# A block kernel's long convolution: transforms split into even and odd tokens, half of the frequencies multiplied, the tables in one ring chunk

## The reference

```python
def hyena_branch(cols, p):
    w = p['hy_conv_w']
    u = w[0] * shift_prev(cols) + w[1] * cols + w[2] * shift_next(cols) + p['hy_conv_b']
    x0, x1, v = jnp.split(u, 3, axis=-1)
    z = v * x1
    z = long_conv(z, hyena_filter_spectrum(cols.shape[1], p)) + p['hy_bias'] * z
    return z * x0

def long_conv(z, spec):
    L = z.shape[1]
    zf = jnp.fft.rfft(z.astype(jnp.float32), n=2 * L, axis=1)
    return jnp.fft.irfft(zf * spec, n=2 * L, axis=1)[:, :L].astype(z.dtype)
```

## Time and profile before

| what | us |
|---|---|
| median of three runs | 3726.84 (3725.3 to 3729.33) |
| span of the profiled execution | 3725.3 |
| time of the fastest run | 3725.3 |
| TensorE busy | 3401.7 (91%) |
| VectorE busy | 1142.7 (31%) |
| ScalarE busy | 599.9 (16%) |
| start of the filter-spectrum matmuls | 798.80 |
| start of the first matmul of `mix_branches` | 887.93 |
| DMA rate in the expert stage | 417 GB/s mean |

### The profile page before, as it was taken

One profiled execution on the slowest core, in us unless ns is written; L12 is line 12 of the kernel. 1 busy time (PEld: TensorE's weight loads), 2 busy tenths in 40 slices (PEclk: granted clock), 3 DMA queues, 4 the chain that ended last, 5 costly groups with the idle time before them and its releaser, 6 DMA issues. The chain is left out here.

```text
span 3725.3 us, 48323 instructions
## 1 busy us (share of the span) xinstructions
PE 3401.7 (91%) x21329; PEld 1687.3 (45%) x21329; DVE 1142.7 (31%) x1977; ACT 599.9 (16%) x1192; POOL 8.0 (0%) x40
## 2 busy tenths in 40 slices
PE   6978999999996988889899899999999977999998
PEld 3557878444444333323333344454444444444443
DVE  2255565432113000000000226644665032222211
ACT  2134322110011000000000212242121012211100
POOL 0000000000000000000000000000000000000000
PEclk9989999999997999999999999999999988999999
DMA  6134444211226999999999521103433234212220
GB/s 239 45 125 169 149 162 162 87 45 45 90 76 269 430 429 431 430 430 428 427 427 430 205 72 63 51 7 80 144 121 138 80 110 162 86 68 68 69 95 34
DMA packets 197654, 668.77 MB, mean 180 GB/s; under 512 B 31048, under 2 KB 95036, under 8 KB 171205
## 3 DMA queue, kind: packets, MB, share of 16 engines
q1 hardware_dynamic: 196456, 665.31, 45.8%
q10 hardware_dynamic: 989, 0.36, 0.0%
HBM read 640.97 MB, written 22.31 MB: 178 GB/s over the span
## 5 line engine op out<-in xcount | busy, mean ns | idle before, releaser
L2718 PE MATMUL banks<-h_T,weight_ring 128*128 128x512 f32 x1408 | 612.7, 596 | 5.9 <-PEq L90 5.9
L2718 PEld LDWEIGHTS banks<-h_T,weight_ring 128*128 128x128 f32 x1408 | 267.5, 191 | 337.7 <-issue 337.7
L2020 PE MATMUL banks<-weight_ring,xe_T 128*64 128x512 f32 x1312 | 296.9, 599 | 41.3 <-DMA weight_ring<-in_exp_w 39.4
L2730 PE MATMUL banks<-weight_ring,ffn_act 128*128 128x512 f32 x704 | 302.5, 592 | 0.0
L2816 DVE SCALAR_TENSOR_TENSOR conv<-banks,cols,conv 128x510 f32<-128x510 f32 (+1 forms) x176 | 131.8, 749 | 341.2 <-ACT conv L2786 336.6
L2730 PEld LDWEIGHTS banks<-weight_ring,ffn_act 128*128 128x128 f32 x704 | 133.8, 190 | 168.4 <-issue 168.4
L2020 PEld LDWEIGHTS banks<-weight_ring,xe_T 128*64 128x64 f32 x1312 | 90.2, 137 | 235.2 <-issue 160.0
L2036 PE MATMUL banks<-weight_ring,hid_T 128*64 128x512 f32 x656 | 146.7, 596 | 9.5 <-DMA weight_ring<-in_exp_w 9.5
L2786 ACT ACTIVATE conv<-banks,cols 128x512 f32<-128x512 f32 x88 | 63.6, 772 | 503.3 <-PE banks L2718 503.3
L2341 PE MATMUL banks<-h_T,weight_ring 128*128 128x512 f32 x320 | 142.0, 597 | 0.0
L2020 PE MATMUL banks<-h_T,xe_T 128*64 128x512 f32 x464 | 105.4, 596 | 17.7 <-DMA h_T<-in_exp_w 17.7
(11 more groups left out here) (579 smaller groups left out, 4135.3 us busy)
## 6 DMA issues: line engine op xcount, KB each, us to landing
weight_ring<-in_exp_w SPq DMA_DIRECT2D x123, 2048.0 KB, 15.7
h_T<-in_exp_w SPq DMA_DIRECT2D x41, 2048.0 KB, 15.7
weight_ring<-in_ada_w SPq DMA_DIRECT2D x24, 2048.0 KB, 8.7
weight_ring<-in_ffn_w_up SPq DMA_DIRECT2D x44, 1024.0 KB, 6.3
expert_out<-in_exp_w SPq DMA_DIRECT2D x19, 2048.0 KB, 19.0
weight_ring<-in_mod_w SPq DMA_DIRECT2D x12, 2048.0 KB, 8.5
weight_ring<-in_ffn_w_down SPq DMA_DIRECT2D x10, 2048.0 KB, 7.8
spare<-in_exp_w SPq DMA_DIRECT2D x9, 2048.0 KB, 20.5
```

Source lines behind the costliest of these rows:

```text
L2020: mm = pe.matmul(k.ps[64 * half:64 * half + 64, 2 * c + b % 2, :], R.rows[:, e // 2 % 2, kt, (e % 2) * CAP:(e % 2 + 1) * CAP], w[:, r, 512 ...
L2718: mm = pe.matmul(k.ps[:, b + c, :], w[:, c, kt, m * P:m * P + P], hT[:, kt, :], start=kt == 0, stop=kt == 7)
L2730: return pe.matmul(k.ps[:, 2 * t + n, :], out[:, kt, t * P:t * P + P], src[:, n * 512:n * 512 + 512], start=kt == 0, stop=kt == FF_T - 1)
```

## The change

The tokens are sorted into even and odd ones. A transform's values at a frequency and at its mirror image differ only in the sign with which the odd tokens enter, so the matmuls are done for the lower 256 frequencies alone, for even and odd tokens apart, and sums and differences of the two parts give both halves.

- **Tables**: `k_dft` has 256 frequencies instead of 512, its rows (and those of the window and the features) in the order even tokens, odd tokens; `k_inverse` has 256 rows. Together they fill one chunk of 2 MB, so the stage takes 4 chunks instead of 5 and every later chunk moves up by one.
- **TensorE**: `half_sums` does 4 parts (cosine even, sine odd, cosine odd, sine even) x 2 tiles of tokens = 8 matmuls for each of 2 tiles of frequencies, for the filter and for z. The transposes read every second token. `back` does the inverse with 256 columns per matmul, even and odd output tokens apart, part of it while VectorE is still at the second tile of frequencies.
- **ScalarE** copies two banks at a time (`crossed`), for the filter and now also for z.
- **VectorE** makes sums and differences (spectrum, `z_parts`), scales, and does the products in `multiply`, on halves of the channels: first the two products' parts, then the sums and differences that the even and the odd half of the inverse need. The output is written in two interleaved halves per channel tile.
- **Banks**: the projection uses banks 0 to 3 (before 0, 2, 4, 6), the filter's network 4 to 7. The chunk of tables is given back when the last inverse matmul is done (before: `k_dft` after the products, `k_inverse` at the end).

The core of the diff (left out: the numbering of the events, and the new bank numbers of the projection, the network and the norm):

```diff
-    w = TWO_PI * (np.arange(L)[None, :] + 0.5) / (2 * L)
-    cos, sin = np.cos(w * n), np.sin(w * n)
+    w = TWO_PI * (np.arange(L // 2)[None, :] + 0.5) / (2 * L)
+    split = np.concatenate([np.arange(0, L, 2), np.arange(1, L, 2)])
+    cos, sin = np.cos(w * n)[split], np.sin(w * n)[split]
...
-        "k_inverse": f(np.stack([cos.T / L, -sin.T / L])), "k_window": f(window),
-        "k_feat": f(feat.T), "k_misc": f(misc), "k_pick": f(pick),
+        "k_inverse": f(np.stack([cos.T / L, -sin.T / L])), "k_window": f(window[split]),
+        "k_feat": f(feat.T[:, split]), "k_misc": f(misc), "k_pick": f(pick),
...
-    out += [[(I["k_dft"][c].rearrange("(k p) n -> p k n", p=P), [P, 4, 512]) for c in range(2)]]
-    out += [[(I["k_inverse"][c].rearrange("(k p) n -> p k n", p=P), [P, 4, 512]) for c in range(2)]]
+    out += [[(I["k_dft"][c].rearrange("(k p) n -> p k n", p=P), [P, 4, 256]) for c in range(2)] +
+            [(I["k_inverse"][c].rearrange("(k p) n -> p k n", p=P), [P, 2, 512]) for c in range(2)]]
...
-    bank = lambda i: 2 * (i % 4)
+    bank = lambda i: i % 4
...
-        spec = sb("filter_spectrum", [P, 2, LT, HY_W])
+        spec = sb("filter_spectrum", [P, 2, 4, HY_W])
+        Z, Q = sb("z_spectrum", [P, 4, HY_W]), sb("spectrum_products", [P, 4, HY_W])
-        ztok, sumdif, prod, scr, window = u[:, 4:8, :], filt, filt, absum, spec[:, 0, :, :]
+        ztok, sumdif, scr, window = u[:, 4:8, :], filt, absum, spec[:, 0, :, :]
+        prod, crossed = filt, absum
+        first_banks, late_banks = (4, 5, 6, 7), (0, 1, 2, 3)
...
-            k.ring.load_ahead(sync, 5)
+            k.ring.load_ahead(sync, 4)
...
-            dft = k.ring.chunk(3).rearrange("p (c t n) -> p c t n", c=2, t=LT)
+            dft = k.ring.chunk(3)[:, 0:2048].rearrange("p (c t n) -> p c t n", c=2, t=LT)
+            inv = k.ring.chunk(3)[:, 2048:4096].rearrange("p (c k n) -> p c k n", c=2, k=2)
+            def half_sums(kt, banks, source):
+                for b, (c, odd) in zip(banks, ((0, 0), (1, 1), (0, 1), (1, 0))):
+                    for t in range(2):
+                        mm = pe.matmul(k.ps[:, b, :], dft[:, c, 2 * odd + t, kt * P:kt * P + P], source(c, 2 * odd + t), start=t == 0, stop=t == 1)
+                return mm
             pe.wait_ge(dve_done, dve_n[("sumdif", LT - 1)])
-            order = (1, 3, 5, 7, 0, 2, 4, 6)
-            for c in range(2):
-                for kt in range(LT):
-                    if c:
-                        pe.wait_ge(dve_done, dve_n[("sums", 8 + kt)])
-                    for t in range(LT):
-                        mm = pe.matmul(k.ps[:, order[4 * c + kt], :], dft[:, c, t, kt * P:kt * P + P], sumdif[:, c, t, :],
-                                       start=t == 0, stop=t == LT - 1)
-                    ev(("spectrum", c, kt), mm)
+            ev(("spectrum", 0), half_sums(0, first_banks, lambda c, t: sumdif[:, c, t, :]))
             pe.wait_ge(dve_done, dve_n[("z", HY_T - 1)])
+            ev(("spectrum", 1), half_sums(1, late_banks, lambda c, t: sumdif[:, c, t, :]))
+            pe.wait_ge(dve_done, dve_n[("spectrum", 0)])
             for t in range(LT):
-                pe.wait_ge(act_done, act_n[("spectrum", 0, t)])
                 for j in range(HY_T):
-                    mm = pe.transpose(k.ps[:, order[t], j * P:j * P + P], u[:, 8 + j, t * P:t * P + P], k.sq("eye"))
+                    mm = pe.transpose(k.ps[:, first_banks[t], j * P:j * P + P], u[:, 8 + j, bass.DynSlice(t // 2 + 256 * (t % 2), P, step=2)], k.sq("eye"))
                 ev(("turned", t), mm)
+            pe.wait_ge(dve_done, dve_n[("spectrum", 1)])
             pe.wait_ge(act_done, act_n[("turned", LT - 1)])
-            for kt in range(LT):
-                for c in range(2):
-                    for t in range(LT):
-                        mm = pe.matmul(k.ps[:, (order[4:] + order[:4])[2 * kt + c], :], dft[:, c, t, kt * P:kt * P + P], ztok[:, t, :],
-                                       start=t == 0, stop=t == LT - 1)
-                ev(("z", kt), mm)
-            k.ring.wait(pe, 4)
-            inv = k.ring.chunk(4).rearrange("p (c t n) -> p c t n", c=2, t=LT)
+            ev(("z", 0), half_sums(0, late_banks, lambda c, t: ztok[:, t, :]))
+            ev(("z", 1), half_sums(1, first_banks, lambda c, t: ztok[:, t, :]))
+            def back(j, kt, odd):
+                for c, part in ((0, 2 * odd), (1, 1 if odd else 3)):
+                    mm = pe.matmul(k.ps[:, j + 4 * odd, 0:256], prod[:, kt, part, j * P:j * P + P], inv[:, c, kt, 256 * odd:256 * odd + 256],
+                                   start=(c, kt) == (0, 0), stop=(c, kt) == (1, 1))
+                return mm
+            for odd in range(2):
+                if odd:
+                    pe.wait_ge(dve_done, dve_n["z_parts_late"])
+                for j in range(HY_T):
+                    pe.wait_ge(dve_done, dve_n[("prod", 0, j // 2)])
+                    back(j, 0, odd)
             for j in range(HY_T):
-                for kt in range(LT):
-                    if j == 0:
-                        pe.wait_ge(dve_done, dve_n[("prod", max(kt, j))])
-                    for c in range(2):
-                        mm = pe.matmul(k.ps[:, order[4 + j], :], prod[:, c, kt, j * P:j * P + P], inv[:, c, kt, :],
-                                       start=(c, kt) == (0, 0), stop=(c, kt) == (1, LT - 1))
-                ev(("y", j), mm)
+                pe.wait_ge(dve_done, dve_n[("prod", 1, j // 2)])
+                back(j, 1, 0)
+                ev(("y", j), back(j, 1, 1))
...
-            for c in range(2):
-                for kt in range(LT):
-                    act.wait_ge(pe_done, pe_n[("spectrum", c, kt)])
-                    ev(("spectrum", c, kt), act.activation(spec[:, c, kt, :], k.ps[:, (1, 3, 5, 7, 0, 2, 4, 6)[4 * c + kt], :], ACT.Copy))
+            crossing = lambda banks: k.ps[:, banks[2]:banks[2] + 2, :]
+            act.wait_ge(dve_done, dve_n[("sumdif", LT - 1)])
+            act.wait_ge(pe_done, pe_n[("spectrum", 0)])
+            ev(("spectrum", 0), act.activation(crossed[:], crossing(first_banks), ACT.Copy))
+            act.wait_ge(pe_done, pe_n[("spectrum", 1)])
+            act.wait_ge(dve_done, dve_n[("spectrum", 0)])
+            ev(("spectrum", 1), act.activation(crossed[:], crossing(late_banks), ACT.Copy))
             for t in range(LT):
                 act.wait_ge(pe_done, pe_n[("turned", t)])
-                ev(("turned", t), act.activation(ztok[:, t, :], k.ps[:, (1, 3, 5, 7)[t], :], ACT.Copy))
+                ev(("turned", t), act.activation(ztok[:, t, :], k.ps[:, first_banks[t], :], ACT.Copy))
+            act.wait_ge(dve_done, dve_n[("spectrum", 1)])
+            act.wait_ge(pe_done, pe_n[("z", 0)])
+            ev(("z", 0), act.activation(crossed[:], crossing(late_banks), ACT.Copy))
+            act.wait_ge(pe_done, pe_n[("z", 1)])
+            act.wait_ge(dve_done, dve_n["z_parts"])
+            ev(("z", 1), act.activation(crossed[:], crossing(first_banks), ACT.Copy))
...
-            for c in range(2):
-                for kt in range(LT):
-                    dve.wait_ge(act_done, act_n[("spectrum", c, kt)])
-                    ev(("scaled", c, kt), dve.tensor_tensor(spec[:, c, kt, :], spec[:, c, kt, :], inv_norm[:], ALU.mult))
-            for kt in range(LT):
-                dve.wait_ge(pe_done, pe_n[("z", kt)])
-                zr, zs = (k.ps[:, (0, 2, 4, 6, 1, 3, 5, 7)[2 * kt + c], :] for c in range(2))
-                hr, hi = spec[:, 0, kt, :], spec[:, 1, kt, :]
-                link(dve.tensor_tensor(scr[:, 0, :], zs, hi, ALU.mult))
-                link(dve.tensor_tensor(scr[:, 1, :], zs, hr, ALU.mult))
-                link(dve.tensor_tensor(prod[:, 0, kt, :], zr, hr, ALU.mult))
-                link(dve.tensor_tensor(prod[:, 1, kt, :], zr, hi, ALU.mult))
-                link(dve.tensor_tensor(prod[:, 0, kt, :], prod[:, 0, kt, :], scr[:, 0, :], ALU.add))
-                ev(("prod", kt), dve.tensor_tensor(prod[:, 1, kt, :], prod[:, 1, kt, :], scr[:, 1, :], ALU.subtract))
-            dve.sem_inc(k.ring.used, 1)
+            direct = lambda banks: k.ps[:, banks[0]:banks[0] + 2, :]
+            for kt, banks in enumerate((first_banks, late_banks)):
+                dve.wait_ge(act_done, act_n[("spectrum", kt)])
+                H = spec[:, kt]
+                dve.tensor_tensor(H[:, 0:2, :], direct(banks), crossed[:], ALU.add)
+                ev(("spectrum", kt), dve.tensor_tensor(H[:, 2:4, :], direct(banks), crossed[:], ALU.subtract))
+                ev(("scaled", kt), dve.tensor_tensor(H, H, bcast(inv_norm[:], 4), ALU.mult))
+            pairs = lambda ap: (ap[:, bass.DynSlice(0, 2, step=2), :], ap[:, bass.DynSlice(1, 2, step=2), :])
+            def z_parts(kt, banks, name):
+                dve.wait_ge(act_done, act_n[("z", kt)])
+                dve.tensor_tensor(Z[:, 0:2, :], direct(banks), crossed[:], ALU.add)
```

(43 more changed lines are left out.)

15 lines of the change are left out of this document (7 added, 8 removed).

## The result

The changed kernel takes 3698.96 us (median of four runs, 3696.78 to 3700.0), the kernel before beside it 3726.07 (four runs, 3721.69 to 3729.33): ratio 0.9921, 95% interval 0.9908 to 0.9934, so 27.1 us less.

A forecast was written before the change was run, and what follows sets the result against it. TensorE was taken to bound the stretch: 41.2 us of matmuls removed, 13.7 given back to VectorE, 2.8 to the clock, leaving 24.7, taken as 24.5. That gave 3700.8, 3702.3 as a median; range 3694 to 3713, own range 3699 to 3706.

The forecast's parts named there:

- TensorE's work: Filter spectrum, transform of z and inverse each lose 13.7 us of matmul time, 41.2 in sum.
- The new wait before z: After the transposes, the transform of z waits about 2.1 us for VectorE, in place of 0.90.
- VectorE sets the end: From z's first results, VectorE's products (5.47 per `multiply`) and outputs set the end; 13.7 given back, gain 27.5 us.
- The barrier: Between hyena's outputs and the mix: VectorE ends at 858.3, the mix starts at 860.4; the earlier trace had 2.08.
- The clock: TensorE's clock falls in the inverse's last two tiles, costing 1.9 us, plus 0.9 at the mix: 2.8 together.
- The edits costing nothing: New bank numbers, one chunk of tables and SyncE's reordered queue cost nothing; the expert stage starts earlier and takes as long.
- The first: Rival: the clock never falls more than before; gain 27.5 us (3697.8), up to 29.3. Chance 14%.
- The second: Rival: the clock falls ahead of the transform of z too; gain 19 to 23 us, 3702 to 3706. Chance 14%.
- The rule of the page: Transposes don't count as TensorE busy, so z's transform would begin at 1.2 GHz; sum 22.7 instead of 24.5 us.
- The third: Rival: matmuls of 256 columns cost as much as 512, slowing inverse and outputs; 3705 to 3709 us. Chance 2%.
- the fourth: Rival: the gain is lost in the expert stage, its loads beginning no earlier; 3725 us. Chance 3%.
- the fifth: Rival: slower, through patterned VectorE instructions in `multiply`; at three times their price 3741.6 us. Chance 2%.

The follow-up runs named there:

- z_twice: Changed kernel with the transform of z computed twice (its 32 records become 64): 3700.74 us, stretch from filter transform to mix 66.65 against 58.72.
- inverse_twice: Changed kernel with 16 more matmuls of 256 columns (6.9 us) in the first half of the inverse: 3696.67 us, stretch 58.78 against 58.72.
- parts_reordered: Changed kernel, doing first those parts of z's transform that need neither the last transposed tile nor VectorE's second difference: 3690.04 us, stretch 57.25 against 58.72.
- linked_products: Changed kernel with each VectorE instruction of `z_parts` and `multiply` waiting for the one before, 18 more links: 3695.5 us, stretch 60.99, 2.27 more.
- returned_late: Changed kernel with the tables' slot given back after the last output instead of ahead of it: 3695.85 us, stretch 59.66, 0.94 more.
- two_chunks: Changed kernel with the tables in two ring chunks of 1 MB again, 5 chunks for the stage: 3691.25 us, stretch 58.85, 0.13 more.
- more_transposes: Changed kernel with the 16 transposes of z done five times (80 records): 3704.56 us, stretch 65.53, 6.81 more.
- filled_lull: Changed kernel with four matmuls that nobody reads between the first output and the barrier: 3699.93 us, stretch 58.74, first mix block 13.81 instead of 15.50.
- changed_again: The changed kernel itself, compared again in five rounds: 3695.32 us against 3725.52 for the kernel before, ratio 0.992, stretch 58.73.
- sums_on_tensor: Changed kernel with two sums of `multiply`, for the first tile of frequencies, left to TensorE (16 more matmuls): 3692.84 us, stretch 56.36, 2.36 less.
- no_final_sums: Changed kernel without the last sum and difference of each `multiply`, so the inverse reads unfinished products: 3686.41 us, stretch 53.40, 5.3 less.

## Why the prediction was right, and where it was short

**The mechanism held.** The time lies 3.3 below the forecast of 3702.3, inside the range, 0.04 under the forecast's own range of 3699 to 3706; the second comparison (3695.32) lies further below. The gain was under-forecast: 24.7 worked out, 30.3 between the two spans. The span was to be 3700.8 and is 3695.0, 5.8 less; the median comes out closer because it lies 4.0 above the span, where 1.5 was added. That part is luck. The likeliest way was the right one, with its clock term too large.

**TensorE's work: right.** 32 records took 13.7 instead of 64 taking 27.5, and the 256-column records are 0.215 apart at full clock. 41.2 went, and z_twice and inverse_twice show which of TensorE's work still counts: that ahead of the first products, and not the inverse.

**The new wait before z: right.** The release is VectorE's second difference, which ends 817.07 - 799.65 = 17.4 after the stage's start where 17.5 was worked out. The wait is 1.67 instead of 2.1, since 16 transposes take 2.07 instead of 1.7. parts_reordered, which removes it, gets 1.47 back.

**VectorE sets the end: right; its pace was mis-sized.** The first sums of z start 25.83 after the stage's start, as worked out (25.8). From there "1.22 + 6 x 0.69, with three linked waits of 0.035" gave 5.47 for one `multiply`, and it measured 5.12; the sums 2.39 instead of 2.48; an output tile 1.64 instead of 1.73. The step added lengths, and unlinked instructions overlap by 0.08. That is 4 x 0.35 + 2 x 0.09 = 1.6 to the end of the products, and 0.3 in the outputs. linked_products shows the effect by itself: 2.27 for 18 links.

**The barrier: wrong by 1.07.** The sum kept the 2.08 of the earlier trace rows between VectorE's last end and the mix. Now it is 858.37 - 857.36 = 1.01. Before, SyncE issued the gate chunk at 885.94, just behind VectorE's end at 885.85, and reached the barrier 1.0 later. The prediction saw that "its 1.0 of issuing ends near 856", and failed to take it out of the 2.08. returned_late puts it back: 0.94.

**The clock: the event right, its price wrong.** The granted clock did fall inside the inverse, and again behind the barrier. Stretches of the changed kernel:

```profile
838.00:842.00 4.00, 3.88 (x10) 3.15 (x11) 3.93 (x5) 0.00 (x0) 0.00 (x0) 0.57 0.01 4
859.00:862.00 3.00, 3.00 (x5) 1.35 (x4) 0.00 (x0) 0.61 (x1) 0.00 (x0) 0.50 1.09 387
862.00:870.00 8.00, 8.00 (x19) 3.42 (x18) 0.00 (x0) 0.00 (x0) 0.00 (x0) 1.00 0.13 46
```

But it fell at 838, not in the last two tiles. The 24 records there take 7.13 instead of 24 x 0.215 = 5.2, TensorE is still early for the next products by 0.37, and VectorE doesn't notice: of the 1.9, nothing is on the path. At the mix the loss is the old one: 15.67 in both kernels. So the 2.8 came to 0.

Together, for the stretch: 1.9 (clock) + 1.6 + 0.3 (VectorE) + 1.07 (barrier) = 4.8 to 4.9. It was to be 89.13 - 27.5 + 1.9 = 63.5, and 58.72 is 4.8 less. The 0.9 for the mix is the rest.

**The edits costing nothing: right.** two_chunks shows it for the layout, the timelines for SyncE's queue and the expert stage; the distance from the mix's start to the end moved by 0.8, within the bound of 3.

**Rivals.** The first (no loss by the clock) named a gain of 27.5. It was right that the clock costs nothing more than before, but for the wrong reason: the clock fell, and it was hidden. That 27.5 lies near the 27.1 between the medians is luck, as the stretch gained 30.4. The second has fallen: the transform of z took 14.00 for 32 records, as the filter's did (13.90). The rule of the page has fallen with more_transposes. The third is excluded by 0.215; the fourth by 2836.6; the fifth by `multiply` at 5.12, with no pattern of 2 x 256 or 4 x 256 slower than a plain one.

**Where the scatter is seen.** In the changed kernel and its variants with one chunk of tables, all code ahead of the filter transform is the same, and yet that transform's first records lie between 795.6 and 803.2. 680 to 690 us, first before, then after:

```profile
680.00:690.00 10.00, 7.50 (x15) 2.24 (x13) 8.47 (x9) 0.27 (x1) 0.00 (x0) 0.88 0.02 5
```

```profile
680.00:690.00 10.00, 7.80 (x13) 2.55 (x12) 7.70 (x8) 0.27 (x1) 0.00 (x0) 0.73 0.01 5
```

So the mean granted clock there differs from run to run. But it doesn't order the starts: z_twice had 0.75 there and its first record is at 797.13, filled_lull 0.88 and 802.49. Over the whole kernel the stretches at 1.2 GHz sum to 244.2 us in the changed kernel's first profile, to 240.8 in changed_again, whose span is 1.7 longer, and to 254.5 in filled_lull. So their sum doesn't explain the time by itself; what does, and why a stretch begins where it does, stays open.

## What to carry to other kernels

When a change takes work from the bounding engine, follow the next engine instruction by instruction from the first result it needs: some 29 of the removed 41.2 us counted (1 more came from the barrier), the rest went to VectorE's chain. Take an engine's pace from start to start, not from lengths, and keep instructions in a row independent of each other where they can be. Split an idle time at a barrier into who comes last and what each engine does just ahead of it; a queue that issues transfers counts too.

## What was not expected of the hardware

- **A link between VectorE instructions costs 0.126 us** (linked_products), since unlinked ones overlap by 0.08 and linked ones leave 0.03; some 0.01 is unexplained. The Trainium skill, page "VectorE: DVE Perf Modes", section "The DRAIN you can't avoid", says of a row of eight tensor_copy that a semaphore after each costs nothing extra. This run disagrees, for fp32 instructions on two tensors where each also waits for the semaphore.
- **A stationary operand read with step two loads slower.** The transposes now read every other token. Weight loads of before and of the changed kernel (count: lowest/median/highest ns):

```profile
L767 PEld LDWEIGHTS banks<-square,hyena_u x16: 139/140/143, 825.8 to 827.8; 128*128 128x128 f32 x16
```

```profile
L773 PEld LDWEIGHTS banks<-square,hyena_u x16: 195/209/209, 813.0 to 815.1; 128*128 128x128 f32 x16
```

  In more_transposes 64 of them take 7.67, 0.120 each, where 0.107 was taken. On VectorE, stride two costs nothing here: the output halves of 256 columns (L916), which read and write every other token, take 0.478, and L2469 with 256 plain columns 0.485.
- **Two DMA issues of SyncE, 1.0 us, delay all engines by 0.94** when they stand just ahead of a barrier (returned_late).
- **A lull's length alone doesn't decide the clock.** Behind 3.91 the mix block took 15.50 from start to start in the changed kernel and 13.81 in parts_reordered; behind 2.76 it took 15.50 in inverse_twice and 13.81 in sums_on_tensor. Nor is the price fixed: behind 3.91 the block took 16.45 in linked_products and 16.58 in z_twice, and 16.83 behind 3.90 in no_final_sums. These losses lie behind the stretch, so no stretch above holds them. What else decides was not settled.
